# Scoring 32 instead of 128 new keys for each running stream, in a one-core attention and mixture-of-experts step

## The chip, the cores and the metric

The kernel runs on one core of one Trainium2 chip. The metric is the device time of one execution in microseconds. A core has five engines that work side by side, each through its own list of instructions: TensorE (PE, matrix products; its weight loads, PEld, overlap the products), VectorE (DVE), ScalarE (ACT), GpSimd (POOL) and SyncE (SP, which issues DMAs).

## What is computed

One inference step of an encoder layer for two groups of tokens with shared weights: a prompt of 256 new frames, and 8 running streams (samples) with 16 new frames each, whose 256 past positions lie in caches. Three attention branches are computed from one input projection, gated, merged and projected; a mixture of 64 small experts follows.

```python
def attend_block(q_nope, q_rope, f_q, c_q, m_q, q_pos, k_nope, k_rope, v_mla, f_k, f_v, c_k, k_pos, m_k, m_v):
    s = (einsum('bqhd,bkhd->bhqk', q_nope, k_nope) + einsum('bqhr,bkr->bhqk', q_rope, k_rope)) * MLA_SCALE
    chunk_mask = (k_pos[None, :] // CHUNK) <= (q_pos[:, None] // CHUNK)
    o_mla = einsum('bhqk,bkhd->bqhd', masked_softmax(s, chunk_mask), v_mla)          # latent branch
    s = einsum('bqhd,bkhd->bhqk', f_q, f_k) * FOX_SCALE
    s = s + (c_q at the query - c_k at the key)                                       # forgetting branch
    o_fox = einsum('bhqk,bkhd->bqhd', masked_softmax(s, k_pos <= q_pos), f_v)
    s = einsum('bqhd,bmhd->bhqm', m_q, m_k) * MEM_SCALE
    o_mem = einsum('bhqm,bmhd->bqhd', softmax(s), m_v)                                # memory branch
```

For a sample the keys of the first two branches are its 256 cached positions and its own 16 new frames.

## The kernel before

All is fp32. The 128 new frames of the 8 samples lie side by side: frame f of sample b is row, or column, 16 b + f of a tile of 128. So does everything made from them: `latT[:, 256:T]` and `krT[:, 256:T]` hold the new latent keys by columns, `latn[:, 2, :]` the same by rows, `fkS` and `fv_tok[:, 2, :]` the new forgetting keys and values.

Attention is cut into units, 64 in all: 32 of the prompt's first two branches, 8 of the prompt's memory branch, and then for each sample b one unit of kind mla (latent), one of fox (forgetting) and one of mem (memory), in that order. A unit has 128 rows, which for a sample are its 16 frames times 8 heads (for mem 4 heads, padded to 32 rows each). A sample's mla and fox units score 384 keys: 256 of the cache and all 128 new ones, of which a mask leaves the sample's own 16. The mask of mla rides in 8 extra rows of `krT` and `qrS`, that of fox is the table `wfox`, added through a product with the identity.

Each unit passes four steps, with these lines:

- scores, on PE: for mla L926 and L927 (cache: latent, rotary part), L928 and L929 (new keys: the same two parts, 128 columns each). For fox L933 (cache) and L935 (new keys), each as four products with 32 weight columns that fill four quarters of the output's partitions, L936 (the forgetting terms, 384 columns) and L938 (the mask). For mem L942.
- maximum (L1768, VectorE), exp (L1420, ScalarE), normalisation (L1776 to L1780, VectorE).
- turning, on PE: one transpose of 128 x 128 for each 128 keys (helper line L889), copied out of PSUM at L1701.
- values, on PE: for mla L963, three products over key tiles; for fox L969, three times four with 32 weight columns; for mem L979. What follows on PE is L1173 for mla, and one more transpose (L889) for fox and mem.

The order is a list, `plan()`, that all engines walk through. At position n stand: the scores of unit n, some gate products (L990, plain 384-column products of a later stage that fill PE's time, spread evenly), the normalisation of n-1, the turning of n-2, the values of n-3 and the follow-up of n-4. The results of turning are so used one position later. SP issues the cache loads for each sample; their waits hang on the units that last used a buffer.

After the units come the merge of the branches (L1183), the output projection (L1192), the router (L1201 and on; its tables of tokens are made at L999, products with 6 columns against full weights) and the experts (L1247 to L1272), whose weights SP streams from HBM.

Of the kernel before, what the change touches and what calls it, by code (L numbers as in the profile page):

```python
# [33 lines left out]
P = 128  # L34
# [5 lines left out]
H, HM = 8, 4  # L40
QL, KVL, RD, ND = 256, 128, 32, 64
CHUNK = 64
E, TOPK, NG, TG = 64, 8, 8, 4
FE = 256

# [105 lines left out]
def units():  # L151

    u = []
    for kind in ("mla", "fox"):
        for two in range(0, H, 2):
            for q in range(2):
                u += [(kind, "p", two, q, P, (q + 1) * P), (kind, "p", two + 1, q, P, (q + 1) * P)]
    for h in range(HM):
        for q in range(2):
            u.append(("mem", "p", h, q, P, NMEM))  # L160
    for b in range(NB):
        u += [("mla", "s", b, 0, P, 3 * P), ("fox", "s", b, 0, P, 3 * P), ("mem", "s", b, 0, P, NMEM)]
    return u


# [107 lines left out]
def build(nc, a, outs):  # L273
# [34 lines left out]
    with ExitStack() as ctx:  # L308
# [287 lines left out]

        def unit_stage(n):

            return U[n][4], U[n][5] // P

        def if_more(eng):

# [268 lines left out]
        def _(pe):  # L871
# [37 lines left out]
            def scores(n):  # L909
                kind, g, i, q, rows, keys = U[n]  # L910
                pe.wait_ge(prep_ready, n + 1)
                out = bank(("S", n))
                if g == "p":
                    qs = slice(q * P, (q + 1) * P)
                    if kind == "mla":
                        last = mm(out[:, 0:keys], qcat[:, i, qs], kcat[:, i, 0:keys], start=True, stop=True)
                    elif kind == "fox":
                        pe.wait_ge(fades_loaded, 32 * H)
                        mm(out[:, 0:keys], fqA[0:66, i, qs], fkA[0:66, i, 0:keys], start=True, stop=False)
                        last = mm(out[:, keys - P:keys], ident, cc("causal"), start=False, stop=True)  # L920
                    else:
                        last = mm(out[:, 0:keys], mqT[:, i, qs], mkT[:, i, :], start=True, stop=True)
                elif kind == "mla":

                    pe.wait_ge(latT_loaded, 32 * (i + 1))
                    mm(out[:, 0:PAST], qabsS[:, i, :], latTc, start=True, stop=False)  # L926
                    mm(out[:, 0:PAST], qrS[0:RD, i, :], krTc[0:RD, :], start=False, stop=True)  # L927
                    mm(out[:, PAST:keys], qabsS[:, i, :], latT[:, 256:T], start=True, stop=False)  # L928
                    last = mm(out[:, PAST:keys], qrS[0:MR, i, :], krT[0:MR, 256:T], start=False, stop=True)  # L929
                elif kind == "fox":  # L930
                    pe.wait_ge(kcache["fk"][i % 2], 16 * (i // 2 + 1))
                    for m in range(4):
                        mm(out[m * 32:(m + 1) * 32, 0:PAST], qbd_fox[:, m, :], fkTc[i % 2][:, m, :], start=True, stop=False)  # L933
                    for m in range(4):
                        mm(out[m * 32:(m + 1) * 32, PAST:keys], qbd_fox[:, m, :], fkS[:, m, :], start=False, stop=False)  # L935
                    mm(out[:, 0:keys], LH[:, 0:P], FR[:, :], start=False, stop=False)  # L936
                    w0 = (7 - i) * NQ
                    last = mm(out[:, PAST:keys], ident, cc("wfox")[:, w0:w0 + P], start=False, stop=True)  # L938
                else:
                    pe.wait_ge(kcache["mk"][i % 2], 16 * (i // 2 + 1))  # L940
                    for m in range(HM):
                        last = mm(out[m * 32:(m + 1) * 32, 0:keys], qbd_mem[:, m, :], mkTc[i % 2][:, m, :], start=True, stop=True)  # L942
                last.then_inc(done["S"], 1)

            def values(n):
# [5 lines left out]
                nk = keys // P  # L951
                if g == "p" and kind != "mem":
                    v = v_mla if kind == "mla" else fv_tok
                    for t in range(nk):
                        for r in range(2):
                            h = i - 1 + r
                            last = mm(out[r * 64:(r + 1) * 64, 0:P], v[:, t, h * 64:(h + 1) * 64], pT[(n - 1 + r) % 3][:, t * P:(t + 1) * P],  # L957
                                      start=(t == 0), stop=(t == nk - 1))
                elif kind == "mla":
                    pe.wait_ge(vcache["lat"][i % 2], 16 * (i // 2 + 1))  # L960
                    for t in range(nk):
                        v = latc[i % 2][:, t, :] if t < 2 else latn[:, 2, :]
                        last = mm(out[:, 0:P], v, pt[:, t * P:(t + 1) * P], start=(t == 0), stop=(t == nk - 1))  # L963
                elif kind == "fox":
                    pe.wait_ge(vcache["fv"][i % 2], 16 * (i // 2 + 1))
                    for t in range(nk):
                        for m in range(4):
                            v = fvc[i % 2][:, t, m * P:(m + 1) * P] if t < 2 else fv_tok[:, 2, m * P:(m + 1) * P]
                            last = mm(out[m * 32:(m + 1) * 32, 0:P], pt[:, t * P + m * 32:t * P + (m + 1) * 32], v,  # L969
                                      start=(t == 0), stop=(t == nk - 1))  # L970
                elif g == "p":
                    for t in range(nk):
                        last = mm(out[:, 0:P], mv_tok[:, t, i * P:(i + 1) * P], pt[:, t * P:(t + 1) * P],
                                  start=(t == 0), stop=(t == nk - 1))
                else:
                    pe.wait_ge(vcache["mv"][i % 2], 16 * (i // 2 + 1))
                    for t in range(nk):
                        for m in range(HM):
                            last = mm(out[m * 32:(m + 1) * 32, 0:P], pt[:, t * P + m * 32:t * P + (m + 1) * 32],  # L979
                                      mvc[i % 2][:, t, m * P:(m + 1) * P], start=(t == 0), stop=(t == nk - 1))  # L980
# [54 lines left out]
            for st in PLAN:  # L1035
                ring, key = st[0], st[1:]
                if ring == "T":
# [27 lines left out]
                            last = tr(out[:, m * P:(m + 1) * P], mk_tok[:, j, m * P:(m + 1) * P], P)  # L1065
                    elif key[0] == "p":
                        n = key[1]
                        rows, nk = unit_stage(n)
# [236 lines left out]
        def _(act):  # L1305
# [27 lines left out]
            for st in PLAN:  # L1333
# [78 lines left out]
                    fn(lft[:, 3, :], lft[:, 2, :], ACT.Ln, bias=one).then_inc(lse_ready, 1)  # L1412
                elif ring == "S":
                    n = key[0]
                    rows, nk = unit_stage(n)
# [49 lines left out]
        def _(dve):  # L1465
# [189 lines left out]
            for st in PLAN:  # L1655
                ring, key = st[0], st[1:]
                if ring == "T":
# [36 lines left out]
                            last = V.tensor_copy(oT[:, 2, :, ts], sv[:, :, 0:NQ])  # L1694
                    elif key[0] == "p":
                        n = key[1]
                        rows, nk = unit_stage(n)
                        if n >= 3:
                            dve.wait_ge(done["V"], done_at("V", "o", values_at(U, n - 3)))
                        if rows == P:  # L1700
                            last = V.tensor_copy(pT[n % 3][:, 0:nk * P], src[:, 0:nk * P])  # L1701
                        else:
                            last = V.tensor_copy(pT[n % 3].rearrange("p (t r) -> p t r", t=3)[:, 0:nk, 0:rows],
                                                 src4[:, 0:nk, 0:rows])
                    last.then_inc(free["T"], 1)
                elif ring == "rms":
                    dve.wait_ge(cst_loaded, 16)
# [55 lines left out]
                    ins.then_inc(fades_ready, 1)  # L1763
                elif ring == "S":
                    n = key[0]
                    rows, nk = unit_stage(n)
                    dve.wait_ge(done["S"], n + 1)
                    V.tensor_reduce(mx[0:rows, n:n + 1], ps["S"][n % 2][0:rows, 0:nk * P], AX, ALU.max, negate=True)\  # L1768
                        .then_inc(max_ready, 1)
                elif ring == "norm":  # L1770
                    n = key[0]
                    rows, nk = unit_stage(n)
# [235 lines left out]
```

## Time and profile before

| | us |
|---|---|
| median of 3 runs | 1135.76 |
| lowest, highest | 1135.4, 1136.64 |
| the profiled execution | 1135.26 |
| span of the program in it | 1133.5 |
| PE busy in it | 1104.6 (97%) |
| VectorE, ScalarE busy | 449.1 (40%), 208.8 (18%) |

The profile is of one execution. Its span is the time from the first to the last of the program's instructions; the 1.8 us beside it lie around them. Busy time of PE is partly modelled (the ends of products are), so starts say more than ends. The chain of work tells, piece by piece, what the last instruction had to wait for; where one engine works without a gap, its pieces there are that engine's list with the time that each took end to end. In the chain and in the other views an fp32 product appears as two instructions, a transpose as one: L928 is one product in the code and x2 in the trace, L963 three and x6.

### The profile page before, as it was taken

How to read it: one execution, taken by the hardware profiler on the slowest of the kernel's cores; microseconds unless marked ns; L12 is line 12 of the kernel's file. 1: busy time of each engine (PE TensorE's matmuls, PEld its weight loads, DVE VectorE, ACT ScalarE, POOL GpSimd, SP SyncE). 2: the span in 40 equal slices, each digit the busy share in tenths (PEclk: the TensorE clock that was granted, in tenths of full speed). 3: DMA queues.
4: the chain of work that ended last, by engine and by line, in shares of the span. 5: the costliest groups of instructions: out<-in, count | busy, mean ns of one | idle time of the engine just before them, and what ended most of it. 6: DMA issues, size and time to landing. Idle time of an engine off the chain costs nothing.

```text
span 1133.5 us, 16219 instructions
## 1 busy us (share of the span) xinstructions
PE 1104.6 (97%) x6074; PEld 618.5 (55%) x6074; DVE 449.1 (40%) x1163; ACT 208.8 (18%) x389; POOL 77.3 (7%) x84
## 2 busy tenths in 40 slices
PE   8999999999999999999999999999999999999994
PEld 3455546666666655457555555555555554554551
DVE  0141014445444333256574434424424434434426
ACT  1222116654334200001011011011011011011012
POOL 2100000000000000001014400000000000000000
PEclk9999999999999999999999999999999999999998
DMA  9532265223655588743489999999999999999981
GB/s 325 189 103 74 80 219 181 70 85 127 237 196 182 177 289 336 306 128 108 173 353 371 392 396 401 408 379 385 403 388 392 405 394 391 408 387 389 397 340 58
DMA packets 82886, 312.29 MB, mean 276 GB/s; under 512 B 13032, under 2 KB 26128, under 8 KB 56584
## 3 DMA queue, kind: packets, MB, share of 16 engines
q1 hardware_dynamic: 65136, 278.08, 62.8%
q0 software_dynamic: 6560, 15.65, 4.5%
q10 hardware_dynamic: 11136, 17.83, 4.5%
q8 instruction: 35, 0.57, 0.2%
q14 instruction: 19, 0.16, 0.0%
HBM read 305.46 MB, written 10.95 MB: 279 GB/s over the span
## 4 chain that ended last, share of the span: by engine, by line
PE 95%; DVE 3%; DMA 1%; issue 1%; ACT 0%; SPq 0%; ACTq 0%; DVEq 0%
PE ps_P L1247 20%; PE ps_P L990 11%; PE ps_V L1272 10%; PE ps_V L1261 10%; PE ps_P L898 7%; PE ps_V L1183 5%; PE ps_S L1261 5%; PE ps_P L906 4%; PE ps_V L1192 4%; PE ps_T L1236 3%; PE ps_T L889 2%; PE ps_V L1224 1%; PE ps_P L1031 1%; DMA xT<-x_t 1%; PE ps_S L1254 1%; PE ps_V L957 1%
## 5 line engine op out<-in xcount | busy, mean ns | idle before, releaser
L1247 PE MATMUL ps_P<-arena,branch_out 128*64 128x256 f32 (+1 forms) x2176 | 233.6, 379 | 0.7 <-DVE branch_out L1880 0.7
L1247 PEld LDWEIGHTS ps_P<-arena,branch_out 128*64 128x64 f32 (+1 forms) x2176 | 152.0, 135 | 90.3 <-issue 19.3
L990 PE MATMUL ps_P<-xT,weight_ring 128*128 128x384 f32 x384 | 136.8, 491 | 0.0
L1901 DVE TENSOR_TENSOR branch_out<-branch_out,ps_P 128x256 f32<-128x256 f32 x33 | 13.9, 421 | 286.0 <-PE ps_P L1247 286.0
L1261 PE MATMUL ps_V<-weight_ring,branch_out 128*128 128x512 f32 x264 | 124.1, 592 | 0.0
L1442 ACT ACTIVATE weight_ring<-ps_V,merge 128x512 f32<-128x512 f32 x66 | 45.3, 687 | 414.0 <-PE ps_V L1272 414.0
L1272 PE MATMUL ps_V<-arena,branch_out 128*64 128x512 f32 (+1 forms) x544 | 120.6, 598 | 0.0
L1924 DVE TENSOR_TENSOR x_sb<-x_sb,ps_V 128x512 f32<-128x512 f32 x132 | 90.7, 687 | 17.4 <-PE ps_V L1261 17.4
L990 PEld LDWEIGHTS ps_P<-xT,weight_ring 128*128 128x128 f32 x384 | 68.9, 190 | 37.9 <-issue 2.5
L1272 PEld LDWEIGHTS ps_V<-arena,branch_out 128*64 128x64 f32 (+1 forms) x544 | 34.8, 135 | 77.2 <-issue 60.4
L1261 PEld LDWEIGHTS ps_V<-weight_ring,branch_out 128*128 128x128 f32 x264 | 47.9, 191 | 47.3 <-issue 47.3
L1261 PE MATMUL ps_S<-weight_ring,branch_out 128*128 128x512 f32 x132 | 67.4, 592 | 0.0
L898 PE MATMUL ps_P<-weight_ring,xT 128*128 128x512 f32 (+1 forms) x144 | 61.7, 590 | 5.6 <-DMA xT<-x_t 5.5
L1183 PE MATMUL ps_V<-branch_out,weight_ring 128*128 128x384 f32 x192 | 62.2, 487 | 0.3 <-DVE branch_out L1694 0.3
L1701 DVE COPY merge<-ps_T 128x256 f32<-128x256 f32 (+2 forms) x64 | 27.1, 424 | 69.0 <-PE ps_T L889 68.8
L1183 PEld LDWEIGHTS ps_V<-branch_out,weight_ring 128*128 128x128 f32 x192 | 36.4, 190 | 25.9 <-DVE branch_out L1694 0.8
L1420 ACT ACTIVATE merge<-ps_S,small 128x256 f32<-128x256 f32 (+2 forms) x64 | 30.3, 474 | 108.7 <-DVE small L1768 108.3
L1924 DVE TENSOR_TENSOR x_sb<-x_sb,ps_S 128x512 f32<-128x512 f32 x66 | 45.4, 687 | 11.3 <-PE ps_S L1261 11.3
L898 PEld LDWEIGHTS ps_P<-weight_ring,xT 128*128 128x128 f32 x144 | 28.1, 198 | 38.3 <-issue 30.4
L1880 DVE COPY branch_out<-ps_T 128x512 f32<-128x512 f32 x66 | 42.5, 685 | 4.6 <-PE ps_T L1236 0.2
L906 PE MATMUL ps_P<-xT,weight_ring 128*128 128x384 f32 x128 | 42.6, 490 | 0.0
L1261 PEld LDWEIGHTS ps_S<-weight_ring,branch_out 128*128 128x128 f32 x132 | 25.1, 190 | 31.6 <-issue 31.6
(326 smaller groups left out, 1054.2 us busy)
## 6 DMA issues: line engine op xcount, KB each, us to landing
arena<-w_e_gate SPq DMA_DIRECT2D x68, 1024.0 KB, 8.6
arena<-w_e_up SPq DMA_DIRECT2D x68, 1024.0 KB, 10.5
arena<-w_e_down SPq DMA_DIRECT2D x68, 1024.0 KB, 7.3
weight_ring<-w_in SPq DMA_DIRECT2D x12, 1024.0 KB, 9.2
weight_ring<-w_in ACTq DMA_DIRECT2D x8, 1024.0 KB, 6.7
gates<-arena ACTq DMA_DIRECT2D x24, 192.0 KB, 3.9
arena<-fox_k_t SPq DMA_DIRECT2D x8, 512.0 KB, 4.1
arena<-cache_fox_v SPq DMA_DIRECT2D x8, 512.0 KB, 4.8
```

Of the source, the lines that this page charges most:

```text
L898: last = mm(out[:, 0:w], src[:, k, j * P:(j + 1) * P], slot[:, k % 4, 0:w], start=(k == 0), stop=(k == KD - 1))
L906: last = mm(out[:, 0:T], slot[:, k % 4, m * P:(m + 1) * P], xT[:, k, :], start=(k == 0), stop=(k == KD - 1))
L990: last = mm(out[:, 0:T], slot[:, k % 4, m * P:(m + 1) * P], xT[:, k, :], start=(k == 0), stop=(k == KD - 1))
L1183: last = mm(out[:, 0:T], slot[:, k, m * P:(m + 1) * P], oT[:, br, k, :], start=(k == 0), stop=(k == 3))
L1192: last = mm(out[:, :], yT[:, k, j * P:(j + 1) * P], slot[:, k % 4, :], start=(k == 0), stop=(k == KD - 1))
L1236: last = nc.tensor.transpose(ps["T"][half][:, k * P:(k + 1) * P], xv[:, half * 4 + k, :], ident)
L1247: last = mm(bank[r:r + wide, 0:256], xgT[q][:, k, r:r + wide], w[h][:, k, :], start=(k == 0), stop=(k == KD - 1))
L1261: mm(tiles[k % 3][:, :], back[1 - q][:, (k // 2) * P:(k // 2 + 1) * P], yo[1 - q][:, (k % 2) * 512:(k % 2 + 1) * 512], start=True, stop=Tr ...
L1272: last = mm(ps["V"][half][r:r + wide, :], hidT[:, m, r:r + wide], ew_down[h][:, m, half * 512:(half + 1) * 512], start=(m == 0), stop=(m = ...
L1442: fn(yo[q][:, half * 512:(half + 1) * 512], ps["V"][half][:, :], ACT.Copy, scale=now_info[:, q, 1:2])\
L1880: V.tensor_copy(xgT[par][:, half * 4:half * 4 + 4, :], ps["T"][half][:, :].rearrange("p (k c) -> p k c", k=4)).then_inc(xgT_ready, 1)
L1924: return V.tensor_tensor(xv, xv, tiles[k % 3][:, :], ALU.add)
```

## The change

A sample's mla and fox units take 288 keys instead of 384: the 256 of the cache and a group of 32 new ones, which holds its own 16 frames and those of the neighbouring sample (samples 0 and 1 share group 0, 2 and 3 group 1, and so on; `own_rows`, `own_columns`). The tables and masks are the same, read at these columns. The group's place in its tiles stays: weights and values are read from rows 32 k to 32 k + 31, and the turned scores of the group land there too. Since a transpose of a 32-column piece would put it at row 0, the third transpose becomes a product with the identity as moving operand, with 32 weight columns, into rows 32 k of PSUM. The forgetting terms, one product of 384 columns before, become two, since their columns are no longer next to each other. The copy of the turned scores becomes two for these units.

```diff
-        u += [("mla", "s", b, 0, P, 3 * P), ("fox", "s", b, 0, P, 3 * P), ("mem", "s", b, 0, P, NMEM)]
+        u += [("mla", "s", b, 0, P, PAST + OWN), ("fox", "s", b, 0, P, PAST + OWN), ("mem", "s", b, 0, P, NMEM)]
...
+        def own_rows(n):
+
+            b = U[n][2]
+            return slice(b // 2 * OWN, b // 2 * OWN + OWN)
...
-                    mm(out[:, PAST:keys], qabsS[:, i, :], latT[:, 256:T], start=True, stop=False)
-                    last = mm(out[:, PAST:keys], qrS[0:MR, i, :], krT[0:MR, 256:T], start=False, stop=True)
+                    mm(out[:, PAST:keys], qabsS[:, i, :], latT[:, own_columns(n)], start=True, stop=False)
+                    last = mm(out[:, PAST:keys], qrS[0:MR, i, :], krT[0:MR, own_columns(n)], start=False, stop=True)
...
-                        mm(out[m * 32:(m + 1) * 32, PAST:keys], qbd_fox[:, m, :], fkS[:, m, :], start=False, stop=False)
-                    mm(out[:, 0:keys], LH[:, 0:P], FR[:, :], start=False, stop=False)
-                    w0 = (7 - i) * NQ
-                    last = mm(out[:, PAST:keys], ident, cc("wfox")[:, w0:w0 + P], start=False, stop=True)
+                        mm(out[m * 32:(m + 1) * 32, PAST:keys], qbd_fox[:, m, :], fkS[:, m, own_rows(n)], start=False, stop=False)
+                    mm(out[:, 0:PAST], LH[:, 0:P], FR[:, 0:PAST], start=False, stop=False)
+                    mm(out[:, PAST:keys], LH[:, 0:P], FR[:, own_columns(n)], start=False, stop=False)
+                    w0 = (7 - i) * NQ + own_rows(n).start
+                    last = mm(out[:, PAST:keys], ident, cc("wfox")[:, w0:w0 + OWN], start=False, stop=True)
...
-                        v = latc[i % 2][:, t, :] if t < 2 else latn[:, 2, :]
-                        last = mm(out[:, 0:P], v, pt[:, t * P:(t + 1) * P], start=(t == 0), stop=(t == nk - 1))
+                        r = own if t == 2 else slice(0, P)
+                        v = latc[i % 2][:, t, :] if t < 2 else latn[own, 2, :]
+                        last = mm(out[:, 0:P], v, pt[r, t * P:(t + 1) * P], start=(t == 0), stop=(t == nk - 1))
...
-                            v = fvc[i % 2][:, t, m * P:(m + 1) * P] if t < 2 else fv_tok[:, 2, m * P:(m + 1) * P]
-                            last = mm(out[m * 32:(m + 1) * 32, 0:P], pt[:, t * P + m * 32:t * P + (m + 1) * 32], v,
+                            v = fvc[i % 2][:, t, m * P:(m + 1) * P] if t < 2 else fv_tok[own, 2, m * P:(m + 1) * P]
+                            last = mm(out[m * 32:(m + 1) * 32, 0:P], pt[r, t * P + m * 32:t * P + (m + 1) * 32], v,
...
-                        for t in range(nk):
+                        for t in range(keys // P):
                             last = tr(out[:, t * P:t * P + rows], prob[n % 3][0:rows, t * P:(t + 1) * P], rows)
+                        if keys % P:
+                            last = mm(out[own_rows(n), PAST:PAST + rows], prob[n % 3][0:rows, PAST:keys], ident, start=True, stop=True)
...
-                    fn(prob[n % 3][0:rows, 0:nk * P], ps["S"][n % 2][0:rows, 0:nk * P], ACT.Exp, bias=mx[0:rows, n:n + 1],
+                    fn(prob[n % 3][0:rows, 0:keys], ps["S"][n % 2][0:rows, 0:keys], ACT.Exp, bias=mx[0:rows, n:n + 1],
...
+                        whole = keys // P * P
+                        last = V.tensor_copy(pT[n % 3][:, 0:whole], src[:, 0:whole])
+                        if keys % P:
+                            last = V.tensor_copy(pT[n % 3][own_rows(n), PAST:PAST + P], src[own_rows(n), PAST:PAST + P])
...
-                    V.tensor_reduce(mx[0:rows, n:n + 1], ps["S"][n % 2][0:rows, 0:nk * P], AX, ALU.max, negate=True)\
+                    V.tensor_reduce(mx[0:rows, n:n + 1], ps["S"][n % 2][0:rows, 0:keys], AX, ALU.max, negate=True)\
...
-                    pv = prob[n % 3][0:rows, 0:nk * P]
+                    pv = prob[n % 3][0:rows, 0:keys]
```

What stands on PE for sample 1, from the scores of its mla unit to those of its fox unit, before. Here the shape behind the names is that of the output, and a product counts once.

```order
L926 MATMUL ps_S<-lngb,arena 128x256
L927 MATMUL ps_S<-lngb,arena 128x256
L928 MATMUL ps_S<-lngb,arena 128x128
L929 MATMUL ps_S<-small,arena 128x128
L990 MATMUL ps_P<-xT,weight_ring 128x384 x4
L889 MATMUL ps_T<-cst,merge 128x128 x3
L963 MATMUL ps_V<-merge,lngb 128x128 x3
L889 MATMUL ps_T<-cst,merge 128x128
L933 MATMUL ps_S<-arena,merge 32x256 x4
L935 MATMUL ps_S<-arena,merge 32x128 x4
L936 MATMUL ps_S<-small 128x384
L938 MATMUL ps_S<-cst 128x128
```

The same place in the changed kernel, whose line numbers are higher by 11 to 17:

```order
L939 MATMUL ps_S<-lngb,arena 128x32
L940 MATMUL ps_S<-small,arena 128x32
L1005 MATMUL ps_P<-xT,weight_ring 128x384 x4
L900 MATMUL ps_T<-cst,merge 128x128 x2
L1089 MATMUL ps_T<-cst,merge 32x128
L977 MATMUL ps_V<-merge,lngb 128x128 x3
L900 MATMUL ps_T<-cst,merge 128x128
L944 MATMUL ps_S<-arena,merge 32x256 x4
L946 MATMUL ps_S<-arena,merge 32x32 x4
L947 MATMUL ps_S<-small 128x256
L948 MATMUL ps_S<-small 128x32
L950 MATMUL ps_S<-cst 128x32
```

The new product L1089 stands between the two transposes and the values, and the forgetting terms (L936 before) are L947 and L948.

A little further on PE, the turning of the mla unit ahead of the values of mem, before:

```order
L990 MATMUL ps_P<-xT,weight_ring 128x384 x4
L889 MATMUL ps_T<-cst,merge 128x128 x3
L979 MATMUL ps_V<-arena,merge 32x128 x8
L889 MATMUL ps_T<-cst,merge 128x128
L926 MATMUL ps_S<-lngb,arena 128x256
```

and in the changed kernel:

```order
L1005 MATMUL ps_P<-xT,weight_ring 128x384 x4
L900 MATMUL ps_T<-cst,merge 128x128 x2
L1089 MATMUL ps_T<-cst,merge 32x128
L994 MATMUL ps_V<-arena,merge 32x128 x8
L900 MATMUL ps_T<-cst,merge 128x128
```

Here the product L1089 stands directly ahead of products that also have 32 weight columns. Nothing changes places; the gate products stand where they stood.

## Rows read from the trace of the kernel before

**Rows 1.** The page, its part on engines: busy us, share of the span, instructions.

```profile
PE 1104.6 (97%) x6074; PEld 618.5 (55%) x6074; DVE 449.1 (40%) x1163; ACT 208.8 (18%) x389; POOL 77.3 (7%) x84
```

**Rows 2.** Busy time by window: the sample units, and the expert stage.

```profile
core 0: us, PE busy (x) PEld busy (x) DVE busy (x) ACT busy (x) POOL busy (x), PEclk, DMA share, GB/s
280.00:385.00 105.00, 105.00 (x913) 65.75 (x911) 46.61 (x157) 39.18 (x72) 0.00 (x0) 1.00 0.64 214
560.00:1110.00 550.00, 549.39 (x3366) 292.54 (x3364) 233.76 (x497) 56.23 (x96) 55.71 (x57) 1.00 0.96 385
```

**Rows 3.** Waits of PE, whole program, first row: us in total, times, longest.

```profile
PE ps_P L898 <- DMA xT<-x_t: 5.5, 2, 5.2
```

**Rows 4.** Chain of work, 317 to 332 us: start, us, what (PE instructions).

```profile
317.56 0.43 PE ps_S L926 x2
317.99 0.62 PE ps_S L927 x2
318.62 0.42 PE ps_S L928 x2
319.03 0.41 PE ps_S L929 x2
319.45 1.49 PE ps_P L990 x4
320.94 0.33 PE ps_T L889 x3
321.26 0.67 PE ps_V L963 x6
321.93 0.11 PE ps_T L889
322.04 0.57 PE ps_S L933 x8
322.61 0.22 PE ps_S L935 x8
322.83 0.84 PE ps_S L936 x2
323.67 0.22 PE ps_S L938 x2
323.89 1.29 PE ps_P L990 x4
...
325.40 0.79 PE ps_V L969 x24
326.20 0.57 PE ps_V L1173 x16
...
330.12 0.33 PE ps_T L889 x3
330.45 0.57 PE ps_V L979 x16
331.02 0.26 PE ps_T L889
331.28 0.22 PE ps_S L926
```

**Rows 5.** Chain of work at 564 us: six routing products of 6 columns each.

```profile
563.92 0.57 PE ps_S L999 x6
```

**Rows 6.** Timeline of PE's weight loads at 528 us, for six such products.

```profile
527.92 0.74 PEld L999 LDWEIGHTS ps_S<-merge,branch_out 128*128 128x128 f32 x6 [0.78 <-DVE branch_out L1637]
```

**Rows 7.** The page's group of weight loads at L990: busy us, mean ns; idle before.

```profile
L990 PEld LDWEIGHTS ps_P<-xT,weight_ring 128*128 128x128 f32 x384 | 68.9, 190 | 37.9 <-issue 2.5
```

**Rows 8.** VectorE, 280 to 385 us, by form: busy us, mean ns; idle before.

```profile
L1701 DVE COPY merge<-ps_T 128x384 f32<-128x384 f32 x14 | 7.8, 557 | 19.3 <-PE ps_T L889 19.3
L1701 DVE COPY merge<-ps_T 128x256 f32<-128x256 f32 x9 | 3.8, 424 | 2.5 <-PE ps_T L889 2.5
L1801 DVE COPY merge<-ps_V 128x128 f32<-128x128 f32 x7 | 2.0, 292 | 0.8
```

More of the change, by code:

```diff
@@ L42 @@
 CHUNK = 64
+OWN = 32
 E, TOPK, NG, TG = 64, 8, 8, 4
@@ L597, in unit_stage, with own_columns @@
         def unit_stage(n):
-            return U[n][4], U[n][5] // P
+            return U[n][4], U[n][5]
+        def own_rows(n):
+            b = U[n][2]
+            return slice(b // 2 * OWN, b // 2 * OWN + OWN)
+        def own_columns(n):
+            b = U[n][2]
+            return slice(SEQ + b // 2 * OWN, SEQ + b // 2 * OWN + OWN)
         def if_more(eng):
@@ L950, in values @@
                 pt = pT[n % 3]
-                nk = keys // P
+                nk = -(-keys // P)
+                own = own_rows(n)
                 if g == "p" and kind != "mem":
@@ L966, in values @@
                     for t in range(nk):
+                        r = own if t == 2 else slice(0, P)
                         for m in range(4):
-                            v = fvc[i % 2][:, t, m * P:(m + 1) * P] if t < 2 else fv_tok[:, 2, m * P:(m + 1) * P]
-                            last = mm(out[m * 32:(m + 1) * 32, 0:P], pt[:, t * P + m * 32:t * P + (m + 1) * 32], v,
+                            v = fvc[i % 2][:, t, m * P:(m + 1) * P] if t < 2 else fv_tok[own, 2, m * P:(m + 1) * P]
+                            last = mm(out[m * 32:(m + 1) * 32, 0:P], pt[r, t * P + m * 32:t * P + (m + 1) * 32], v,
                                       start=(t == 0), stop=(t == nk - 1))
@@ L1067, in _ @@
                         n = key[1]
-                        rows, nk = unit_stage(n)
+                        rows, keys = unit_stage(n)
                         pe.wait_ge(norm_ready, n + 1)
                         out = bank(st)
-                        for t in range(nk):
+                        for t in range(keys // P):
                             last = tr(out[:, t * P:t * P + rows], prob[n % 3][0:rows, t * P:(t + 1) * P], rows)
+                        if keys % P:
+                            last = mm(out[own_rows(n), PAST:PAST + rows], prob[n % 3][0:rows, PAST:keys], ident, start=True, stop=True)
                     elif key[0] == "o":
@@ L1414, in _ @@
                     n = key[0]
-                    rows, nk = unit_stage(n)
+                    rows, keys = unit_stage(n)
                     act.wait_ge(max_ready, n + 1)
@@ L1696, in _ @@
                         n = key[1]
-                        rows, nk = unit_stage(n)
+                        rows, keys = unit_stage(n)
                         if n >= 3:
                             dve.wait_ge(done["V"], done_at("V", "o", values_at(U, n - 3)))
[L1700 to L1704, printed above, removed]
+                        whole = keys // P * P
+                        last = V.tensor_copy(pT[n % 3][:, 0:whole], src[:, 0:whole])
+                        if keys % P:
+                            last = V.tensor_copy(pT[n % 3][own_rows(n), PAST:PAST + P], src[own_rows(n), PAST:PAST + P])
                     last.then_inc(free["T"], 1)
@@ L1765, in _ @@
                     n = key[0]
-                    rows, nk = unit_stage(n)
+                    rows, keys = unit_stage(n)
                     dve.wait_ge(done["S"], n + 1)
-                    V.tensor_reduce(mx[0:rows, n:n + 1], ps["S"][n % 2][0:rows, 0:nk * P], AX, ALU.max, negate=True)\
+                    V.tensor_reduce(mx[0:rows, n:n + 1], ps["S"][n % 2][0:rows, 0:keys], AX, ALU.max, negate=True)\
                         .then_inc(max_ready, 1)
@@ L1771, in _ @@
                     n = key[0]
-                    rows, nk = unit_stage(n)
+                    rows, keys = unit_stage(n)
                     dve.wait_ge(exp_ready, n + 1)
```

## The prediction

> **What bounds the kernel now.** I read the page's engine line first [rows 1]: PE (TensorE) is busy for 97% of the span, VectorE for 40%. The change touches only the sample units, which run between about 280 and 385 us. In that window [rows 2] PE is busy for 105.00 of 105.00 us, VectorE for 46.6 and ScalarE for 39.2, at a granted clock of 1.00 (2.4 GHz); in the expert stage, 560 to 1110 us, PE is busy for 549.39 of 550. The table of waits [rows 3] has as its largest row 5.5 us in the whole program, for the first load of x. So in the stage of the change, and behind it, time is what PE's instruction list takes: a microsecond added to or taken from that list should reach the end whole, and one saved on VectorE or ScalarE should not.
>
> The chain of work [rows 4] gives that list piece by piece. One sample (an mla, a fox and a mem unit, with the gate products at L990 between them) repeats every 13.72 us (L926 at 317.56 and at 331.28), eight times. Each product in the code is two PE instructions for fp32 (x2 in the chain), a transpose one. From these rows I take four prices.
>
> - Columns: 256 moving columns cost 0.43/2 = 0.215 us per instruction (L926), 384 cost 1.29/4 = 0.32 (L990), 128 cost 0.67/6 = 0.11 (L963). That is 0.084 us per 100 columns.
> - A change of the shape of array in use. L927 has the same 256 columns as L926 but only 32 weight rows, and takes 0.62 for two instead of 0.43. L928, back at 128 rows, takes 0.42 for two where L963's pace gives 0.22. L936, coming from weights 32 wide, takes 0.84 where 2 x 0.32 = 0.64 is the column time. L990 behind L929 takes 1.49 instead of 1.29. So each entry into a shape with 128 weight columns costs 0.20 us. Entry into 32-wide weights costs 0.13: L979 0.57 for four rounds of 0.11 (four groups side by side), L969 0.79 for six. A transpose behind another shape costs 0.26 instead of 0.11, so 0.15. L935 behind L933, the same shape, pays nothing.
> - Weights: the routing's L999 products move only 6 columns, which would be 0.005 us each, and yet six take 0.57 us [rows 5], and six weight loads start (0.74 - 0.19)/5 = 0.11 apart [rows 6], where 0.19 is the duration of one load of 128 columns [rows 7]. A product with 128 weight columns has a floor of 0.11 us, whatever it moves. 128 moving columns are already at that floor.
> - The last product of a run has no load behind it to wait for, so there the shorter move counts: 0.11 - 0.03 = 0.08 us.
>
> **The change part by part**, per sample.
>
> Scores of mla (L928, L929: 128 columns to 32). Each is a pair on its own shape, with an entry on both sides. The second product still waits for its weights; only its own end is 0.08 earlier. Twice 0.08: -0.16.
>
> Scores of fox. L935 (32-wide weights, four groups): its two rounds move 32 columns instead of 128. The nearest rows are L1173, where 16 instructions with 16 columns take 0.57 - 0.13 = 0.44, 0.027 each; at that pace the eight of L935 would take the 0.22 they take now. The other end is two rounds of 0.03, a saving of 0.16. I take -0.16, because in the 32-wide shape four start together, and 0.027 an instruction at L1173 is also what two 64-wide loads side by side at half of 0.11 would give; the range keeps 0. L936 (384 columns, x2) becomes a 256-column and a 32-column product, two instructions each, and L938's columns go from 128 to 32: before 0.84 + 0.22 = 1.06, after 0.20 + 0.43 + four at the floor of 0.11 = 1.07. That is +0.01: moving columns are exchanged for two more weight loads, and nothing is won.
>
> Turning of the fox unit and values of mla (they stand in one row on PE, with the mem unit's transpose behind them). Before [rows 4]: L889 x3 0.33 + L963 x6 0.67 + L889 0.11 = 1.11. After: two transposes 0.22; then the new product with 32-wide weights, entry 0.13 + 2 x 0.11 = 0.35; four value instructions at 128 x 128, entry 0.20 + 0.45 = 0.65; two with 32 weight rows, entry 0.20 + 0.22 = 0.42; the transpose behind, 0.26. Sum 1.90: +0.79. The third value product is no cheaper for having 32 rows: it has the same 128 weight columns and 128 moving ones, and L927 shows no gain per column from 32 rows. The next piece, L933, pays its 0.13 in either case.
>
> Values of fox (L969). The third tile has 32 weight rows, so there is one entry more, 0.13, and the same instructions: +0.13.
>
> Turning of mla, then values of mem (L889 x3, L979). Before 0.33 + 0.57 = 0.90. After two transposes 0.22, the new product 0.13 + 0.22, and L979 without its entry, since the shape is already 32 wide, 0.44: 1.01. +0.11.
>
> Sum per sample: -0.16 - 0.16 + 0.01 + 0.79 + 0.13 + 0.11 = +0.72 us. Eight samples give 5.8; the first has no mem transpose behind its values, which takes 0.15 off: **+5.6 us**.
>
> VectorE and ScalarE: the maximum, exp and normalisation run over 288 instead of 384 columns and get shorter. The copy out of the turned scores, 0.56 us at 384 columns, becomes one of 256 (0.42) and one of 32 x 128, at most the 0.29 of a 128 x 128 one [rows 8]: up to 0.15 us longer. Both sides I cost at nothing. The cover is PE's own order: the turning at 320.94 is used by values no earlier than the next step, some 4 us on (L969 stands at 325.40 [rows 4]), and VectorE has over half of the window free. If that cover were gone, 16 copies at 0.15 would be 2.4 us. No DMA and no queue is moved; loads whose waits hang on these units come due as much later as their readers.
>
> Against the trace I weigh two rules. The rows show a 32-row or 32-wide shape costing an entry of 0.13 to 0.20. The Trainium skill ("TensorEngine Tiling (Array Packing)", section Tiling Modes) says that changing the tiling mode, not merely the tile, drains the engine; this speaks against the change, which adds five entries per sample, and the trace agrees for every shape that it has, while 32 x 32 and a 32-row shape at rows 32, 64 or 96 are in no row. The Trainium skill ("TensorE: Matmul & The Clock Gate", section Back-to-back issue gap) lists about 60 cycles for any width of 1 to 64 columns, which would make the new products cheaper than my floor; L999 shows 0.11 us at 6 columns, and the same page's section on LDWEIGHTS has the load go by weight columns, as the row does.
>
> The profiled execution took 1135.26 us (span 1133.5), 0.5 below the median of three. I add the sum to both: 1140.9 for an execution like the profiled one, 1135.76 + 5.6 = **1141.4** for the median.
>
> **The rivals.**
>
> Short products go by their columns. Then L928 and L929 are 0.20 + 2 x 0.03 each, saving 0.31 together; L936 and L938 become 0.63 + 4 x 0.03 = 0.75, saving 0.31; with L935 that is -0.78, against +1.03 for the rest: +0.25 a sample, 8 x 0.25 - 0.15 = 1.9 us, 1137.6. For it: the diff cuts columns everywhere. Against it: L999. This is the result that the skill's 60 cycles would give, too.
>
> Thirty-two weight rows at these places need no entry of their own. Values of mla then cost 0.20 + 6 x 0.11, and the sum there is 1.55 instead of 1.90; values of fox +0. Per sample -0.31 + 0.44 + 0.11 = +0.24, in all about 1.9 us (the first sample no different here): 1137.7. For it: no row shows 32 x 32. Against it: L927 and L928, where exactly the number of rows changes.
>
> It is faster: a product costs its moving columns and nothing else, no load floor and no entries. Four products of S mla save 4 x 0.08, L935 0.16, L936 and L938 0.32 together, and the new turning product costs 0.11 twice: -0.58 a sample, -4.6 us, 1131.1. It decides only if both the floor of L999 and the 0.20 entries vanish. Nothing in the rows is for it.
>
> It is slower still: a wait arises that is hidden now, at the longer copy (2.4 us) on top of L935 saving nothing (1.3 us): 1145.1. Against it: 4 us of cover.
>
> **How the numbers follow.** Forecast 0.78. One of the two middle cases 0.13; they are within 0.2% (2.3 us), which is about what a measurement of this kernel can tell from no change. Faster 0.03. Slower still 0.06. So slower by over 0.2% 0.84, same 0.13, faster 0.03. The forecast's own range is 1139.5 to 1143.0 (L935 without gain is +1.3; entries of the new shapes a quarter off are some 1.2 us either way). To leave out no more than 2 in 10 I go down to the middle cases and a little up: 1137.0 to 1143.5.
>
> **What would show it.** In the chain of the changed kernel the period of one sample should be 14.4 us instead of 13.72. L928's successor should take about 0.34 for two, not 0.26; the value product with 32 rows about 0.42 for two, and the four ahead of it 0.65; the 32-column products of fox 0.11 each. PE should still wait for nothing between 280 and 385 us, and everything behind 400 us should be the same piece for piece, shifted. The prediction is wrong if the period does not grow, or if it grows and the expert stage gives the time back.

## The result, and the profile after

The changed kernel takes 1141.35 us (median of 5 runs, 1141.14 to 1141.63) beside 1135.76 (5 runs, 1135.4 to 1136.64): 5.6 us more, a ratio of 1.0047 with a 95% interval of 1.0035 to 1.0058. The profiled execution took 1141.57 us, with a span of 1139.8.

PE is still the bound, and still waits for nothing where the samples are: the window of the changed kernel, with the same columns as [rows 2].

```profile
280.00:385.00 105.00, 105.00 (x885) 66.24 (x884) 44.83 (x163) 36.68 (x66) 0.00 (x0) 1.00 0.63 209
```

In 105 us PE now gets through 885 instructions instead of 913: it is as busy, and slower. The lower figures of VectorE and ScalarE (44.83 and 36.68 us for 46.61 and 39.18) come in part from less of the stage lying in the window. Over the whole program ScalarE has a little less work (207.5 us busy for 208.8) and VectorE a little more (450.1 for 449.1): the shorter maxima, normalisations and copies save less than the sixteen extra copies take (L1720, 32 x 128, 0.285 us each). Neither shows in the time.

The chain of work of one sample in the changed kernel, to be laid beside [rows 4] (start, us, what; L937 to L940 are L926 to L929 of before, L1005 is L990, L900 is L889, L977 is L963, L984 is L969, L994 is L979, L1089 is the new product):

```profile
318.99 0.43 PE ps_S L937 x2
...
320.05 0.34 PE ps_S L939 x2
320.38 0.34 PE ps_S L940 x2
...
322.21 0.22 PE ps_T L900 x2
322.43 0.34 PE ps_T L1089 x2
322.76 1.05 PE ps_V L977 x6
323.81 0.26 PE ps_T L900
...
324.64 0.06 PE ps_S L946 x8
324.70 0.63 PE ps_S L947 x2
325.33 0.14 PE ps_S L948 x2
325.47 0.22 PE ps_S L950 x2
325.70 1.37 PE ps_P L1005 x4
...
327.29 0.92 PE ps_V L984 x24
...
332.13 0.22 PE ps_T L900 x2
332.35 0.23 PE ps_T L1089
332.58 0.03 PE ps_V L994 x3
332.61 0.08 PE ps_T L1089
332.69 0.44 PE ps_V L994 x13
333.12 0.26 PE ps_T L900
333.38 0.43 PE ps_S L937 x2
```

The step from one sample to the next is 333.38 - 318.99 = 14.39 us instead of 13.72, +0.67. By parts, after less before (the parts are rounded one by one and add up to 0.69):

- Scores of mla: 0.34 + 0.34 for 0.42 + 0.41, -0.15.
- Scores of fox, the new keys: L946 0.06 for 0.22, -0.16.
- Scores of fox, forgetting terms and mask: L947, L948 and L950 take 0.63 + 0.14 + 0.22 = 0.99, where L936 and L938 took 0.84 + 0.22 = 1.06. The gate products behind them take 1.37 instead of 1.29, since the first of them now waits for its weights (its load starts 0.03 us ahead of it, at 325.50, and before 0.11 us ahead, at 323.62). Together 0.99 + 0.08 = 1.07 for 1.06, +0.01.
- Turning of fox with values of mla and the transpose behind (L900, L1089, L977, L900): 0.22 + 0.34 + 1.05 + 0.26 = 1.87 for 1.11, +0.76. This is the one large term.
- Values of fox: 0.92 for 0.79, +0.13.
- Turning of mla with values of mem: 0.22 + 0.23 + 0.03 + 0.08 + 0.44 = 1.00 for 0.90, +0.10.

To see the whole stage I take, in every kernel, the time from the start of the first sample's first score product to the start of the first product of the merge. Before and after (of the second line of each only the start counts, since the piece is cut off where the view ends):

```profile
276.96 0.43 PE ps_S L926 x2
...
398.07 7.04 PE ps_V L1183 x21
```

```profile
277.07 0.43 PE ps_S L937 x2
...
403.77 1.24 PE ps_V L1200 x3
```

That is 121.11 us before and 126.70 after: +5.59, the whole of the 5.6 between the medians. What the sample units add is passed on in full. The two profiled spans differ by more (6.3 us): 0.1 lies at the start, and 0.6 behind the merge, where no line of the program was changed. These 0.6 arise at one place of the expert stage: an expert's first products (L1264, L1247 before) start 5.72 us later than before up to the one at 608.70 us, and 6.30 us later from the next, at 626.82, to the last. Between them PE waits 0.3 us for an addition on VectorE (L1917), which it doesn't before. What made that addition late isn't shown; the medians differ by no more than the stage.

### The profile page after: what moved, and what is told of

Same layout as the page of the kernel before. It is cut to its first block, busy times and chain, and to the rows that moved or that the text cites. A ratio compares the mean times of both kernels' runs of the same rounds, so it can differ in the third digit from the quotient of the medians.

```text
span 1139.8 us, 16299 instructions
## 1 busy us (share of the span) xinstructions
PE 1109.6 (97%) x6106; PEld 621.4 (55%) x6106; DVE 450.1 (39%) x1179; ACT 207.5 (18%) x389; POOL 77.6 (7%) x84
## 4 chain that ended last, share of the span: by engine, by line
PE 95%; DVE 3%; DMA 1%; issue 1%; ACT 0%; SPq 0%; ACTq 0%; DVEq 0%
PE ps_P L1264 20%; PE ps_P L1005 11%; PE ps_V L1289 10%; PE ps_V L1278 10%; PE ps_P L909 7%; PE ps_V L1200 5%; PE ps_S L1278 5%; PE ps_P L917 4%; PE ps_V L1209 4%; PE ps_T L1253 3%; PE ps_T L900 2%; PE ps_V L1241 1%; PE ps_P L1046 1%; DMA xT<-x_t 1%; PE ps_V L977 1%; PE ps_S L1271 1%
## 5 line engine op out<-in xcount | busy, mean ns | idle before, releaser
L1264 PE MATMUL ps_P<-arena,branch_out 128*64 128x256 f32 (+1 forms) x2176 | 233.6, 379 | 0.7 <-DVE branch_out L1896 0.7
L1264 PEld LDWEIGHTS ps_P<-arena,branch_out 128*64 128x64 f32 (+1 forms) x2176 | 152.0, 135 | 90.3 <-issue 19.3
L1005 PE MATMUL ps_P<-xT,weight_ring 128*128 128x384 f32 x384 | 137.5, 492 | 0.0
L1917 DVE TENSOR_TENSOR branch_out<-branch_out,ps_P 128x256 f32<-128x256 f32 x33 | 13.9, 422 | 286.8 <-PE ps_P L1264 286.8
L1005 PEld LDWEIGHTS ps_P<-xT,weight_ring 128*128 128x128 f32 x384 | 68.9, 191 | 37.3 <-issue 2.9
L1718 DVE COPY merge<-ps_T 128x256 f32<-128x256 f32 (+1 forms) x64 | 25.0, 391 | 75.1 <-PE ps_T L900 48.3
```

The costliest lines, as they stand in the source:

```text
L1005: last = mm(out[:, 0:T], slot[:, k % 4, m * P:(m + 1) * P], xT[:, k, :], start=(k == 0), stop=(k == KD - 1))
L1264: last = mm(bank[r:r + wide, 0:256], xgT[q][:, k, r:r + wide], w[h][:, k, :], start=(k == 0), stop=(k == KD - 1))
```

## Experiments

Seven kernels were run. Their times are compared with runs of the kernel before on the same chip at the same time (median 1135.29 for e1_scores, e2_values, e3_turn and e5_pair, 1135.51 for e4_split, e7_full and e8_both). The first score product of the samples starts at 276.7 to 277.4 us in most of them and at 278.15 in e3_turn (the first loads, and what a kernel clears there), so the stage as measured above says more than the total, and stands beside it.

The expectations speak of theory A: a product with 128 weight columns takes at least 0.11 us, and each change of array shape (an "entry") costs 0.13 to 0.20 us. The rivals B (short products go by their columns) and C (32 rows are no shape of their own) are the prediction's two middle cases.

### The scores alone (e1_scores)

The changed kernel with turning and values as they were. Exp writes the 32 columns back to their place in a tile whose other columns are kept at zero, in a second instruction with a second sum:

```diff
-                    fn(prob[n % 3][0:rows, 0:keys], ps["S"][n % 2][0:rows, 0:keys], ACT.Exp, bias=mx[0:rows, n:n + 1],
-                       accum_out=sm[0:rows, n:n + 1]).then_inc(exp_ready, 1)
+                    last = fn(prob[n % 3][0:rows, 0:whole], ps["S"][n % 2][0:rows, 0:whole], ACT.Exp, bias=mx[0:rows, n:n + 1],
+                              accum_out=sm[0:rows, n:n + 1])
+                    if keys % P:
...
+                        last = fn(prob[n % 3][:, PAST + r.start:PAST + r.stop], ps["S"][n % 2][:, PAST:keys], ACT.Exp,
+                                  bias=mx[:, n:n + 1], accum_out=rs[:, n:n + 1])
...
-                        for t in range(keys // P):
+                        for t in range(-(-keys // P)):
                             last = tr(out[:, t * P:t * P + rows], prob[n % 3][0:rows, t * P:(t + 1) * P], rows)
-                        if keys % P:
-                            last = mm(out[own_rows(n), PAST:PAST + rows], prob[n % 3][0:rows, PAST:keys], ident, start=True, stop=True)
```

> The change's scores alone: 32 new columns are scored, exp writes them back to their place among 128 (its other 96 columns are kept zero), and turning and values are those of the kernel before. Theory A (a product with 128 weight columns has a floor of 0.11 us, an entry into another array shape costs 0.13 to 0.20 us): L928 and L929 save 0.08 each, L935 0.16, L936 and L938 nothing, 0.31 to 0.32 us a sample, 2.5 us in all: 1133.2 if before is 1135.8. Rival B (short products go by their columns): 0.78 a sample, 6.2 us: 1129.6. Rival D (the gain at the end of a run of short products isn't there): 1135.8. The second exp and the added sum on ScalarE and VectorE cost nothing by every theory.

Measured: 1133.78 us for 1135.29, ratio 0.9986 (0.9977 to 0.9995). The stage takes 118.64 us, -2.47, as theory A has it. The chain shows the sizes of the changed kernel in the scores, and those of the kernel before in what follows:

```profile
318.09 0.34 PE ps_S L939 x2
318.43 0.34 PE ps_S L940 x2
...
320.25 0.33 PE ps_T L900 x3
320.58 0.67 PE ps_V L975 x6
...
321.93 0.06 PE ps_S L946 x8
```

The total falls by 1.5 us only, a microsecond less than the stage. Of this 0.4 lies ahead of the stage, whose first product starts at 277.36 us instead of 276.96. There the two tiles are cleared on VectorE just ahead of the first score product of all, which waits for VectorE for 1.2 us instead of 0.7. Another 0.2 lies behind the stage. The rest lies outside the span: every execution of this kernel is 2.1 to 2.3 us longer than its span, every one of the kernel before 1.8 to 1.9. The same holds for e3_turn (2.2) and e8_both (2.1 to 2.2) and for none of the others; why, no run shows.

### The values alone (e2_values)

```diff
-                        v = latc[i % 2][:, t, :] if t < 2 else latn[:, 2, :]
-                        last = mm(out[:, 0:P], v, pt[:, t * P:(t + 1) * P], start=(t == 0), stop=(t == nk - 1))
+                        r = own_group(n) if t == 2 else slice(0, P)
+                        v = latc[i % 2][:, t, :] if t < 2 else latn[r, 2, :]
+                        last = mm(out[:, 0:P], v, pt[r, t * P:(t + 1) * P], start=(t == 0), stop=(t == nk - 1))
```

(and the same for fox).

> The change's values alone: the kernel before, but the third key tile's products of mla and fox take only the 32 rows of the sample's group. Theory A: entries alone. After mla's four full instructions one entry of 0.20 into the 32-row shape and one of 0.15 for the transpose behind (none behind the first sample's), and one of 0.13 in fox: 0.48 a sample, less 0.15 once, +3.7 us: 1139.5. Rival C (32 weight rows are no shape of their own at these places): 0, 1135.8. If 32 rows were cheaper per column it would be below 1135.8.

Measured: 1138.80 us for 1135.29, ratio 1.0033 (1.0021 to 1.0044); the stage 124.74, +3.63. Theory A had 3.7. Reading a quarter of the rows costs time and saves none. The chain of this kernel:

```profile
321.82 0.86 PE ps_V L968 x6
322.68 0.26 PE ps_T L893
...
326.31 0.93 PE ps_V L975 x24
```

L968 is 0.86 for 0.67, the transpose behind it 0.26 for 0.11, and fox's L975 0.93 for 0.79. That 32 rows at these places are no shape of their own, one of the middle cases of the prediction, is ruled out.

### The turning alone (e3_turn)

```diff
-                        for t in range(nk):
+                        for t in range(min(nk, 2)):
                             last = tr(out[:, t * P:t * P + rows], prob[n % 3][0:rows, t * P:(t + 1) * P], rows)
+                        if nk == 3:
+                            r = own_group(n)
+                            last = mm(out[r, PAST:T], prob[n % 3][:, PAST + r.start:PAST + r.stop], ident, start=True, stop=True)
```

> The change's turning alone: the kernel before, but the third tile's transpose of mla and fox is a product with 32 weight columns onto the group's rows, copied apart, with the other rows of the tile kept zero; scores and values are full. Theory A: in fox an entry of 0.13, one of 0.20 back to the values' shape and one instruction more (0.11): 0.44; in mla 0.11, since the values of mem that follow are in the same shape: 0.55 a sample, +4.4 us: 1140.2. Rival (entries cost nothing here, only the second instruction counts): 0.22 a sample, +1.8 us: 1137.6. Rival (the two copies on VectorE are what the changed kernel paid for): PE would show waits at the values, and the period of a sample would grow by them.

Measured: 1141.29 us for 1135.29, ratio 1.0049 (1.0035 to 1.0062); the stage 125.53, +4.42, where theory A said 4.4. The total says no more than that it is close: from the second sample on a step grows by 0.50 to 0.52 instead of 0.55, and the first sample costs 0.3 more than I had counted, for the reason given further below, so the two misses cancel. Of the rest of the 6.0 us, 1.2 lies ahead of the stage, whose first product starts at 278.15 us instead of 276.96, and 0.4 outside the span. Ahead of the stage PE waits 0.5 us longer for VectorE, which again clears tiles there, and in the profiled execution 1.1 us longer for the first load of x; that is more than 1.2 together, and what took the rest back isn't shown. No wait of PE stands in the stage, so the longer way over VectorE (two copies and at times a clearing) costs nothing there.

```profile
323.57 0.22 PE ps_T L893 x2
323.79 0.34 PE ps_T L1079 x2
324.13 0.86 PE ps_V L967 x6
```

The six value instructions are the full ones (they have all 128 rows), yet they take 0.86 for 0.67: the entry back into their shape.

The three parts are -2.47 + 3.63 + 4.42 = +5.58 in the stage, and the whole change is +5.59. Nothing is left over for an effect of the parts on each other.

### Entries taken away (e5_pair, e7_full)

If entries are what costs, taking them away from the kernel before must give time back, with the same products. In the first of these kernels mla's score products stand in another order (the two with 128 rows first), and the cache's rotary part gets 8 rows of zeros, so that both rotary products have 40 rows:

```diff
                     mm(out[:, 0:PAST], qabsS[:, i, :], latTc, start=True, stop=False)
-                    mm(out[:, 0:PAST], qrS[0:RD, i, :], krTc[0:RD, :], start=False, stop=True)
-                    mm(out[:, PAST:keys], qabsS[:, i, :], latT[:, 256:T], start=True, stop=False)
+                    mm(out[:, PAST:keys], qabsS[:, i, :], latT[:, 256:T], start=False, stop=False)
+                    mm(out[:, 0:PAST], qrS[0:MR, i, :], krTc[0:MR, :], start=False, stop=False)
                     last = mm(out[:, PAST:keys], qrS[0:MR, i, :], krT[0:MR, 256:T], start=False, stop=True)
```

> Entries taken away instead of added: the kernel before with mla's four score products in another order, the two with 128 weight rows first, then the two rotary ones, both with 40 rows (the cache's rotary part is padded with 8 zero rows). Same products, same columns. Theory A: four entries in a sample (into 32 rows, back to 128, into 40, back to 128) become two, 0.40 us a sample, -3.2 us: 1132.6. Rival (the 0.20 is the time of products with few rows, wherever they stand): 0, 1135.8. Rival B says nothing of it: 0.

Measured: 1132.53 us for 1135.29, ratio 0.9971 (0.9960 to 0.9982); the stage 117.99, -3.12.

```profile
329.63 0.43 PE ps_S L926 x2
330.07 0.22 PE ps_S L927 x2
330.29 0.63 PE ps_S L928 x2
330.91 0.22 PE ps_S L929 x2
331.13 1.49 PE ps_P L990 x4
```

Here L927 is the product of 128 rows and 128 columns that took 0.42 in [rows 4] behind one of 32 rows; behind one of its own shape it takes 0.22. L929, with 40 rows behind 40 rows, takes 0.22 for 0.41. The time hangs on the neighbour, not on the product.

In the second the order is the same, and all four have 128 rows; what isn't content is zero:

```diff
+                    mm(out[:, 0:PAST], qrS[:, i, :], krTc, start=False, stop=False)
+                    last = mm(out[:, PAST:keys], qrS[:, i, :], krT[:, 256:T], start=False, stop=True)
...
+            nc.gpsimd.memset(qrS[RD:64], 0.0).then_inc(rows_set, 1)
+            nc.gpsimd.memset(krT[RD:64, 256:T], 0.0).then_inc(rows_set, 1)
...
+            nc.gpsimd.memset(qrS[64:P], 0.0).then_inc(rows_set, 1)
+            nc.gpsimd.memset(krT[64:P, 256:T], 0.0).then_inc(rows_set, 1)
+            nc.gpsimd.memset(krTc[RD:64], 0.0).then_inc(rows_set, 1)
+            nc.gpsimd.memset(krTc[64:P], 0.0).then_inc(rows_set, 1)
```

> All entries of mla's scores taken away: the kernel before, with both rotary products on 128 weight rows (the rows without content are zero, in weights and keys), so that the four products and their neighbours have one shape. Theory A: four entries of 0.20 a sample go, -6.4 us: 1128.9 beside 1135.3. Rival (products with more rows cost more): less than that, or slower. The rows are cleared by GpSimd in the first 15 us, which should cost nothing.

Measured: 1128.95 us for 1135.51, ratio 0.9947 (0.9933 to 0.9961); the stage 114.89, -6.22. Theory A had -6.4. Multiplying by 88 or 96 rows of zeros is free, and leaving them out cost 6 us:

```profile
315.01 0.43 PE ps_S L932 x2
315.44 0.22 PE ps_S L933 x2
315.67 0.43 PE ps_S L934 x2
316.10 0.22 PE ps_S L935 x2
316.32 1.29 PE ps_P L996 x4
```

The new order also ends that two products in a row add to the same columns of PSUM. That this was the gain is a rival that falls by rows already shown: the three products of L963 add to the same columns and take 0.11 us an instruction, and L928 pays its 0.20 behind L927, which writes other columns.

What an entry is made of can be seen in the timeline of the weight loads of the kernel before:

```profile
317.92 0.29 PEld L927 LDWEIGHTS ps_S<-lngb,arena 32*128 32x128 f32 x2 [0.33 <-issue]
```

The first load for the 32-row shape starts no earlier than its product (317.92 both), after 0.33 us in which no weights were loaded. In e7_full, where the shape stays, the load of L933 starts at 315.07, 0.21 us ahead of its product at 315.28, under the product before. So at a change of shape the load isn't hidden. How much of the 0.20 us is the load and how much something else isn't measured.

### The floor of a short product (e4_split)

The kernel before, with the mask product of fox in four pieces of 32 columns:

```diff
-                    last = mm(out[:, PAST:keys], ident, cc("wfox")[:, w0:w0 + P], start=False, stop=True)
+                    for c in range(4):
+                        last = mm(out[:, PAST + c * 32:PAST + c * 32 + 32], ident, cc("wfox")[:, w0 + c * 32:w0 + c * 32 + 32],
+                                  start=False, stop=(c == 3))
```

> The floor of a short product by itself: the kernel before, with the mask product of fox (L938, 128 columns) cut into four of 32 columns, eight instructions for two, the same columns and the same result. Theory A (0.11 us for every product with 128 weight columns): 0.22 becomes 0.88 a sample less 0.08 at the end of the run, +0.58, +4.6 us in all: about 1139.9 beside 1135.3. Rival B (by columns): no change, or up to 0.1 a sample.

Measured: 1141.25 us for 1135.51, ratio 1.0046 (1.0031 to 1.0062); the stage 126.46, +5.35. The same columns in four times as many products cost nearly four times as much:

```profile
325.05 0.84 PE ps_S L936 x2
325.89 0.81 PE ps_S L939 x8
326.70 1.37 PE ps_P L992 x4
```

0.81 + 1.37 for 0.22 + 1.29 is +0.67 a sample (L939 is the mask product in its four pieces, L938 before). I had expected 0.58: I took 0.08 off for the end of the run, but behind the run stand products of the same shape, and the first of them waits for its weights in place of the last one. By this and by e8_both below, the end of a run saves time only where the shape changes behind it. With this, the other middle case of the prediction (short products go by their columns) is ruled out.

### A version that beats both (e8_both)

The scores on 32 columns as in the first experiment, mla's four score products on 128 rows as in e7_full, and the clearing of the two tiles at a place where VectorE has time.

```diff
+                    mm(out[:, PAST:keys], qabsS[:, i, :], latT[:, own_columns(n)], start=False, stop=False)
+                    mm(out[:, 0:PAST], qrS[:, i, :], krTc, start=False, stop=False)
+                    last = mm(out[:, PAST:keys], qrS[:, i, :], krT[:, own_columns(n)], start=False, stop=True)
```

> The version that should beat both: the scores on 32 new columns (as when the scores were changed alone) and mla's four score products all on 128 rows. Theory A says that the two gains don't add: with no entry behind them, L928 and L929 with 32 columns stand at the floor of 0.11 that they have with 128 columns, and only L935's 0.16 is left of the 32 columns: -0.80 - 0.16 a sample, -7.7 us: 1127.6 beside 1135.3. Rival (gains add, -6.4 and -2.5): 1126.4. In the chain the four products should take 0.22 each for the two of 32 columns by A, and 0.06 by B. The clearing of the two score tiles stands at a later place than before, where VectorE has time.

Measured: 1128.01 us for 1135.51, ratio 0.9936 (0.9923 to 0.9950); the stage 113.72, -7.39, where theory A had -7.7. It is the fastest of all, 13 us below the changed kernel. Beside e7_full it gains 1.17 us in the stage and 0.9 in the median. The gains don't add (-6.22 - 2.47 would be -8.7):

```profile
314.62 0.43 PE ps_S L943 x2
315.05 0.14 PE ps_S L944 x2
315.19 0.51 PE ps_S L945 x2
315.71 0.14 PE ps_S L946 x2
315.85 1.37 PE ps_P L1008 x4
```

The chain doesn't give the 0.22 apiece that I had written for the two short products, but 0.14, with the missing 0.08 at the next piece each time: 0.51 for 0.43, 1.37 for 1.29. The five pieces are 2.59 us, as in e7_full (2.59). For mla's score products, all in one shape, 32 columns are worth nothing against 128.

## Why the prediction was right

The forecast was 1141.4 us, and 1141.35 was measured. The mechanism was the one forecast: entries added on PE's list, and no gain from fewer columns but at a few ends. By its own steps:

- PE's list is the time, and a microsecond in it goes through: right. The stage grew by 5.59, the medians by 5.6; PE waits for nothing in the stage; in e1_scores the exp in two instructions and the extra sum leave no trace in it. The longer way over VectorE was sized rightly, too (sixteen copies of 0.285 us), and cost nothing.
- "Repeats every 13.72 us, eight times" was a wrong reading of the chain, without effect on the sum. Before, only three of the seven steps from sample to sample are 13.72; two are 15.02, with four more instructions of L990 in them, and the first two 11.97 and 13.61. What the sum needs is the growth of a step, and that is even: 0.67 or 0.68 in each of the last five.
- Scores of mla -0.16: -0.15. The 0.08 that the shorter move of a product's second instruction brings is there because each of the two products has a change of shape behind it; e8_both shows it gone when that change is gone.
- L935 -0.16 with 0 as the other end: -0.16. The choice between far bounds was right. L1173's 0.027 an instruction was not the pace of instructions: eight of L946 take 0.06.
- The floor of 0.11 as the time of a weight load: held, by e4_split. [rows 7] has loads of one width only; that a load goes by its weight columns and not by its rows, other loads of the kernel before show: 0.190 us for 128 columns (L990), 0.137 for 64 (L1173), 0.110 for 32 (L935), and 0.183 for 128 columns with only 32 rows (L927).
- The forgetting terms and the mask +0.01: +0.01, through two pieces of which I had the sum right and the split not: 0.36 and 0.08 at the successor instead of four times 0.11.
- Turning of fox and values of mla +0.79: +0.76. Values of fox +0.13: +0.13. Turning of mla +0.11: +0.10.
- The step that failed is a small one, the turning of mla in the first sample. I took 0.15 off for the missing transpose of mem, and overlooked that the first sample's turned mla unit is followed by the values of a prompt unit (L973, L988 in the changed kernel), with 128-wide weights. So there the new product does pay for its entry and for the one back. Chain of the changed kernel:

```profile
287.96 0.22 PE ps_T L900 x2
288.18 0.34 PE ps_T L1089 x2
288.52 0.64 PE ps_V L988 x4
```

The same place takes 0.33 + 0.45 before, so it is +0.42 and not +0.11. The sum by measured parts is 8 x 0.69 - 0.15 + 0.32 = 5.7, for 5.59 measured (the parts' rounding, 0.69 for steps that grow by 0.67, is the difference); mine was 8 x 0.72 - 0.15 = 5.6. Per sample I was 0.03 to 0.05 too high and for the first one 0.3 too low, and the two cancel: the last tenths of the agreement are luck.

The rivals: that short products go by their columns falls with e4_split, that 32 rows have no entry falls with e2_values, and both together were what a faster kernel needed. A slower one through the copies didn't come: e3_turn, with more VectorE work than the change (453.0 us busy for 450.1), has no PE wait in the stage.

The shapes that no row of before had cost their entries, too: 32 x 32 in L984 (0.92 for 0.79), and 32 rows by 128 at every place, since L977 takes 1.05 in all eight samples, from rows 0 to 31 (at 294.22 us) to rows 96 to 127 (at 394.11). The Trainium skill ("TensorEngine Tiling (Array Packing)", section Tiling Modes) says that a change of the tiling mode drains the engine. The traces agree in that every change of shape whose price can be read in the chains costs time, 0.13 to 0.20 us; that it is a draining they don't show.

## What to carry to other kernels

Count a list of small products by three things before cutting their columns: weight loads, moving columns, and changes of array shape. In this fp32 kernel, cutting the columns of a product with 128 weight columns below 128 saved nothing (its weights take 0.11 us an instruction), unless the shape changed right behind it, where it saved 0.08 us. A cut in rows that changed the shape cost 0.13 to 0.20 us an entry and saved nothing; filling rows with zeros to keep one shape was worth 6 us. Where a short product has to have another shape, put it beside others of that shape: behind the new product L1089, the values of mem pay no entry (0.03 + 0.44 for 0.57).

## What the runs showed that I had not expected

Four products of 32 weight columns side by side, with 32 moving columns, take 0.06 us for eight instructions (L946), 0.008 each, while L1173 with 64 weight columns and 16 moving ones takes 0.027 each, if its entry is taken as 0.13. So the issue of instructions doesn't bind at 0.027, and the floor of 0.11 an instruction was met with 128 weight columns only. What sets L1173's pace stays open. And the order of mla's score products, with eight rows of zeros added to one of them and nothing computed otherwise, was worth 3 us.
